# Prompt attention in one straight list with scores two steps ahead, weights and values changing places on TensorE, and DeltaNet's ScalarE work in one activation table

## What is computed

```python
def stick_breaking_block(q, k, v, q_pos, k_pos):
    z = einsum('bqhd,bshd->bhqs', q, k) * HEAD_DIM ** -0.5
    valid = k_pos[None, :] < q_pos[:, None]
    log_keep = where(valid, log_sigmoid(-z), 0)
    log_rest = cumsum(log_keep, axis=3, reverse=True) - log_keep
    a = where(valid, exp(log_sigmoid(z) + log_rest), 0)
    return einsum('bhqs,bshd->bqhd', a, v)

def trunk_layer(...):
    proj = rmsnorm(x, g_mix) @ w_in
    c = silu(causal_conv(dn_qkv));  qa, ka, va = split(c)
    qa = l2norm(qa) * HEAD_DIM ** -0.5;  ka = l2norm(ka)
    o_a, s_new = gated_delta_rule(qa, ka, va, g, beta, s0)     # in blocks along the tokens
    o_a = rmsnorm(o_a, g_out_dn) * silu(z)
    o_b = stick_breaking(rmsnorm(sb_q), concat(k_past, rmsnorm(sb_k)), concat(v_past, sb_v))
    h = x + concat(o_a, o_b) @ w_out
    h = h + square(relu(rmsnorm(h) @ w_up)) @ w_down
    return h + sigmoid(rmsnorm(h) @ w_ple_gate) * (p @ w_ple_proj)
```

## Time and profile before

| | us |
|---|---|
| median of 3 runs | 2249.35 (2248.25 to 2250.07) |
| profiled execution | 2247.63 |
| its span, first to last instruction | 2245.9 |
| prompt attention, first L1587 to first L1636 | 436.5 to 676.7 |
| DeltaNet, chunk loop and ends | about 737 to 1222 |
| one attention pair, scores at 501.75 to scores at 559.96 | 58.2 |
| one DeltaNet chunk, the load before Ln at 846.79 to the same at 901.54 | 54.75 |
| granted TensorE clock, mean | 0.944 |

### The profile page before, as it was taken

One profiled execution on the slowest core, in us unless ns is written; L12 is line 12 of the kernel. 1 busy time (PEld: TensorE's weight loads), 2 busy tenths in 40 slices (PEclk: granted clock), 3 DMA queues, 4 the chain that ended last, 5 costly groups with the idle time before them and its releaser, 6 DMA issues.

```text
span 2245.9 us, 32884 instructions
## 1 busy us (share of the span) xinstructions
PE 2010.0 (89%) x13793; PEld 1867.9 (83%) x13793; DVE 893.9 (40%) x1069; ACT 556.1 (25%) x926; POOL 607.6 (27%) x239
## 2 busy tenths in 40 slices
PE   5999999776775699999998999999999999999699
PEld 4899899644543488888887999999999999999577
DVE  5550336366662366666563152122221222225421
ACT  4231132345454233333332031001010010103210
POOL 5213323000001433333320233434334343343100
PEclk9999999888788799999997999999999999999899
DMA  5022211200004200000002011111111111111101
GB/s 166 20 76 73 82 67 57 86 1 1 1 1 155 67 20 20 19 19 19 19 9 86 20 57 38 41 36 56 56 37 43 33 56 56 37 51 47 64 28 39
DMA packets 90868, 104.16 MB, mean 46 GB/s; under 512 B 9492, under 2 KB 74336, under 8 KB 90784
## 3 DMA queue, kind: packets, MB, share of 16 engines
q1 hardware_dynamic: 81440, 89.96, 12.5%
q10 hardware_dynamic: 9344, 12.98, 1.6%
HBM read 85.32 MB, written 17.60 MB: 46 GB/s over the span
## 4 chain that ended last, share of the span: by engine, by line
PE 81%; DVE 6%; ACT 6%; issue 2%; DMA 2%; POOL 2%; SPq 0%; ACTq 0%; DVEq 0%; POOLq 0%
PE psum L1542 43%; PE psum L1514 4%; PE psum L1515 4%; PE psum L1516 4%; PE psum L1814 3%; PE psum L1818 3%; PE psum L1803 2%; PE psum L1587 2%; PE psum L1611 2%; PE psum L1737 2%; PE psum L1600 2%; DVE area L1255 1%; PE psum L1590 1%; DVE area L1160 1%; ACT area L903 1%
## 5 line engine op out<-in xcount | busy, mean ns | idle before, releaser
L674 POOL TENSOR_TENSOR w_hi<-w_raw,ones 128x2048 fp32r<-128x2048 f32 x51 | 184.7, 3622 | 1132.6 <-PE psum L1542 622.8
L1542 PE MATMUL psum<-act_hi,w_hi 128*128 128x352 f32 x1248 | 270.0, 324 | 0.6 <-ACT area L1039 0.6
L1542 PE MATMUL psum<-act_hi,w_lo 128*128 128x352 f32 x1248 | 268.9, 323 | 0.0
L1542 PE MATMUL psum<-act_lo,w_hi 128*128 128x352 f32 x1248 | 268.6, 323 | 0.0
L675 POOL TENSOR_TENSOR w_lo<-w_raw,w_hi 128x2048 fp32r<-128x2048 f32 x51 | 255.2, 5004 | 4.0
L1514 PE MATMUL psum<-w_hi,act_hi 128*128 128x256 f32 (+1 forms) x720 | 225.9, 314 | 28.2 <-issue 17.2
L1515 PE MATMUL psum<-w_lo,act_hi 128*128 128x256 f32 (+1 forms) x720 | 221.5, 308 | 0.0
L1516 PE MATMUL psum<-w_hi,act_lo 128*128 128x256 f32 (+1 forms) x720 | 220.4, 306 | 0.0
L1394 DVE TENSOR_TENSOR area<-psum,area 128x1056 f32<-128x1056 f32 x72 | 90.5, 1257 | 317.3 <-PE psum L1542 317.3
L1542 PEld LDWEIGHTS psum<-act_hi,w_lo 128*128 128x128 f32 x1248 | 214.2, 188 | 0.0
L1542 PEld LDWEIGHTS psum<-act_hi,w_hi 128*128 128x128 f32 x1248 | 212.4, 189 | 0.7 <-ACT area L1039 0.7
(11 more groups left out here) (268 smaller groups left out, 3082.1 us busy)
## 6 DMA issues: line engine op xcount, KB each, us to landing
w_raw<-in_w_up_dram SPq DMA_DIRECT2D x16, 1024.0 KB, 5.5
w_raw<-in_w_down_dram SPq DMA_DIRECT2D x16, 1024.0 KB, 5.0
w_raw<-in_w_in_dram SPq DMA_DIRECT2D x14, 1024.0 KB, 5.5
area<-in_x_prompt_dram SPq DMA_DIRECT2D x16, 512.0 KB, 4.0
conv_scratch<-area ACTq DMA_DIRECT2D x12, 512.0 KB, 2.6
area<-conv_scratch SPq DMA_DIRECT2D x8, 768.0 KB, 4.5
w_raw<-in_cache_k_dram SPq DMA_DIRECT2D x2, 2048.0 KB, 8.7
area<-in_cache_v_dram SPq DMA_DIRECT2D x2, 2048.0 KB, 8.4
```

The source lines that it names most:

```text
L674: own.link(pool.tensor_tensor(hi, w_raw[:, slot, :], ones[:, 0:1].to_broadcast([P, BLK]), ALU.mult))
L1542: last = pe.matmul(bank(base + c)[0:rows, 0:CH], w(k), a[:, k, CH * c:CH * (c + 1)], start=(k == 0 and w is lhs_hi and a is hi), stop=(k = ...
```

## The change

- The loop over pairs is gone: `STEPS` is one list of 32 (pair, tile) steps, the same tile order in each pair, written out on all engines. Semaphores count on from 0, without the 1 added at the start.
- Scores are made two steps ahead. TensorE's order is turn(s, 0), scores(s+2), values(s-1), turn_out(s-2), turn(s, 1). ScalarE's is copies(s, 0), sigmoids(s+2, 0), copies(s, 1), sigmoids(s+2, 1), copy_out(s-1). The score banks, the ring buffers and at_buf keep their size.
- In the value product the attention block is the weight matrix (128x128) and 64 columns of values stream; the output is token-major. ScalarE copies it to SBUF (`copy_out`, two buffers), TensorE transposes it (`turn_out`) into the other columns of its bank, VectorE splits that.
- DeltaNet: the table set with both Exp and Ln is loaded ahead. One over the square root in `output` is Ln and Exp on ScalarE in place of Sqrt and VectorE's reciprocal. The Exp that ends the key norm writes PSUM banks 4 and 5 in place of SBUF, and `unit_norms` reads it there.

```diff
+        ORDER = [t for n in range(NT // 2) for t in (n, NT - 1 - n)]
+        STEPS = [(i, t) for i in range(WT) for t in ORDER]
...
+        out_buf = [o_buf.rearrange("p g d -> p (g d)"), ab_raw[:, :, :].rearrange("p k c -> p (k c)")]
...
...
+            def sigmoids(step, u):
+                w = P * (STEPS[step][1] + 1)
+                act.wait_ge(scores_ready, step + 1)
+                if step >= 2:
+                    act.wait_ge(att_turned, 2 * (step - 2) + u + 1)
...
+            def copy_weights(step, u):
+                if step:
+                    act.wait_ge(o_ready, step)
                 for n, lo, hi in pieces_of(step, u):
+                    act.wait_ge(turned, n + 1)
                     act.activation(at_buf[:, u, lo:hi], bank(4 + n % 2)[:, 0:hi - lo], ACT.Copy).then_inc(att_placed, 1)
+            def copy_out(step):
+                act.wait_ge(o_ready, step + 1)
+                if step >= 2:
+                    act.wait_ge(o_turned, step - 1)
+                act.activation(out_buf[step % 2], bank(6 + step % 2)[:, 0:P], ACT.Copy).then_inc(o_copied, 1)
+            for step in range(2):
+                for u in range(2):
+                    sigmoids(step, u)
+            for step in range(len(STEPS)):
+                for u in range(2):
+                    copy_weights(step, u)
+                    if step + 2 < len(STEPS):
+                        sigmoids(step + 2, u)
+                if step:
+                    copy_out(step - 1)
+            copy_out(len(STEPS) - 1)
...
-                act.activation(rs, rs, ACT.Exp, scale=-0.5).then_inc(sd2_made, 1)
+                act.activation(head_banks(4, P, n), rs, ACT.Exp, scale=-0.5).then_inc(sd2_made, 1)
...
-                act.activation(small[0:n, 8:16], small[0:n, 0:8], ACT.Sqrt, scale=1.0 / HD,
-                               bias=eps[0:n, :]).then_inc(osd_made, 1)
+                own.link(act.activation(small[0:n, 8:16], small[0:n, 0:8], ACT.Ln, scale=1.0 / HD, bias=eps[0:n, :]))
+                act.activation(small[0:n, 48:56], small[0:n, 8:16], ACT.Exp, scale=-0.5).then_inc(osd_made, 1)
...
+            act.preload_act_table_set("natural_log_exp_and_others")
...
...
+            def split_out(step):
+                i, t = STEPS[step]
+                dve.wait_ge(o_turned, step + 1)
+                src = bank(6 + step % 2)[:, P:2 * P]
...
+            for step in range(len(STEPS)):
+                for u in range(2):
...
+                    dve.wait_ge(sig_made, 2 * step + u + 1)
...
+                if step >= 2:
+                    split_out(step - 2)
...
-                tt(d_cn[:, :, 0:n], d_c[:, 0:KT, 0:n], d_rs[:, :, 0:n], ALU.mult).then_inc(cn_made, 1)
+                tt(d_cn[:, :, 0:n], head_banks(4, P, n), d_c[:, 0:KT, 0:n], ALU.mult).then_inc(cn_made, 1)
...
-                own.link(dve.reciprocal(small[0:n, 48:56], small[0:n, 8:16]))
...
...
+            def scores(step):
...
+                if step:
+                    pe.wait_ge(sig_made, 2 * step)
...
+            def values(step):
+                i, t = STEPS[step]
+                pe.wait_ge(att_placed, pieces_of(step, 1)[-1][0] + 1)
+                if step >= 2:
+                    pe.wait_ge(o_split, step - 1)
+                for u in range(2):
+                    for n in range(t + 1):
+                        last = pe.matmul(bank(6 + step % 2)[:, HD * u:HD * (u + 1)], at_buf[:, u, P * n:P * (n + 1)],
                                          v_tok[:, n, P * i + HD * u:P * i + HD * (u + 1)],
-                                         at_buf[:, u, P * n:P * (n + 1)], start=(n == 0), stop=(n == t))
+                                         start=(n == 0), stop=(n == t))
                 last.then_inc(o_ready, 1)
...
+            def turn_out(step):
+                pe.wait_ge(o_copied, step + 1)
+                pe.transpose(bank(6 + step % 2)[:, P:2 * P], out_buf[step % 2], ident[:]).then_inc(o_turned, 1)
+            scores(0)
+            scores(1)
+            for step in range(len(STEPS)):
+                turn_weights(step, 0)
+                if step + 2 < len(STEPS):
+                    scores(step + 2)
+                if step:
+                    values(step - 1)
+                if step >= 2:
+                    turn_out(step - 2)
+                turn_weights(step, 1)
```

More of the change, by code:

```diff
@@ L447, in token_banks @@
             return psum[:, b:b + 2, :].rearrange("p a (k t) -> p (a k) t", k=4)[:, :, 0:rows]
-        UNITS = 2 * NT
-        STEPS = [t for n in range(NT // 2) for t in (n, NT - 1 - n)]
-        PIECES = 3 * NT
+        ORDER = [t for n in range(NT // 2) for t in (n, NT - 1 - n)]
+        STEPS = [(i, t) for i in range(WT) for t in ORDER]
         def columns_of(step):
-            t = STEPS[step]
+            t = STEPS[step][1]
             if t < NT // 2:
@@ L1021, in _ @@
             with act.Fori(0, (NT - 2) // 2) as i:
+                own.enter(i, 2)
                 for u in range(2):
@@ L1026, in _ @@
                     last_level(2 * i + u + 1, 1 - u)
+                own.leave((NT - 2) // 2)
             first_level(NT - 1, P)
@@ L1207, in split_out @@
                 own.link(dve.tensor_copy(dst, src))
[L1208 to L1224, removed]
+                dve.tensor_tensor(act_lo[:, WT + i, cols], src, dst.bitcast(F32), ALU.subtract).then_inc(o_split, 1)
@@ new lines, in _ @@
+            for step in range(len(STEPS)):
+                for u in range(2):
+                    w = P * (STEPS[step][1] + 1)
+                    keep, sig = keep_buf[:, u, columns_of(step)], sig_buf[:, u, columns_of(step)]
+                    dve.wait_ge(sig_made, 2 * step + u + 1)
+                    back = keep[:, ::-1]
+                    own.link(dve.tensor_tensor_scan(back, back, back, 1.0, ALU.mult, ALU.min))
+                    dve.tensor_tensor(sig[:, 0:w - 1], sig[:, 0:w - 1], keep[:, 1:w], ALU.mult).then_inc(att_made, 1)
+                if step >= 2:
+                    split_out(step - 2)
@@ L1226, in _ @@
+            split_out(len(STEPS) - 2)
+            split_out(len(STEPS) - 1)
             for g in range(2):
@@ L1603, in turn_weights @@
                 pe.sem_inc(att_turned, 1)
[L1605 to L1611, removed]
+            def values(step):
+                i, t = STEPS[step]
+                pe.wait_ge(att_placed, pieces_of(step, 1)[-1][0] + 1)
[4 more added lines that the diff above has]
+                        last = pe.matmul(bank(6 + step % 2)[:, HD * u:HD * (u + 1)], at_buf[:, u, P * n:P * (n + 1)],
                                          v_tok[:, n, P * i + HD * u:P * i + HD * (u + 1)],
-                                         at_buf[:, u, P * n:P * (n + 1)], start=(n == 0), stop=(n == t))
+                                         start=(n == 0), stop=(n == t))
                 last.then_inc(o_ready, 1)
[L1616 to L1627, removed]
+            def turn_out(step):
[12 more added lines that the diff above has]
+                turn_weights(step, 1)
+            values(len(STEPS) - 1)
+            turn_out(len(STEPS) - 2)
+            turn_out(len(STEPS) - 1)
+            pe.wait_ge(o_split, WT * NT)
             pe.wait_ge(s_staged, 4)
```

43 lines of the change are left out of this document (11 added, 32 removed).

## The result

| | before | after |
|---|---|---|
| median | 2249.61 (4 runs) | 2343.43 (2337.54 to 2347.11, 4 runs) |
| profiled execution | 2247.63 | 2345.43 |
| its span | 2245.9 | 2343.7 |
| granted TensorE clock, mean | 0.944 | 0.92 |

The ratio is 1.0416, with a 95% interval of 1.0392 to 1.0439: slower by 4.2%, some 94 us, where 40 were forecast. The time lies above the range of 2232 to 2338.

What follows compares the result with a forecast made beforehand. The prediction took waits between three engines, none full, to bound prompt attention and DeltaNet. Profiled 2247.63, + 82 for attention - 41 for DeltaNet, gave 2288.6, a median of 2290 us; range 2232 to 2338.

Steps and rivals of the forecast that it cites:

- the clock's share: Prompt attention: 0.45 of TensorE's 31.2 us of chain work a pair is paid extra for half clock, 14.0 us.
- the sum of waits: Prompt attention at full clock: 19.3 + 18.45 + 12.05 + 15.6 = 65.4 us a pair, four pairs 261.6.
- What waits for what: Prompt attention: each step lasts the larger of ScalarE's and VectorE's branches, plus scores and values in full.
- the second branch: Prompt attention: value products, turned output, split, scan, multiply, turn, scores form a chain, 18.45 us a pair in small-tile steps.
- The price of the value product: Prompt attention: 0.216 us each with attention block as weight, against 0.12 before; 72 a pair, 15.6 us against 8.9.
- VectorE's queue: Prompt attention: split_out(s-2) waits for the turned output and stands before the scans of step s+1.
- Added copy and transposition at nothing: Prompt attention: the copy of an output, 0.2 us, lies hidden under scores and values.
- DeltaNet, 41 us: DeltaNet: 5.2 us saved a chunk in seven chunks, 4.3 in the first, none in the last; bounds 28 and 51.
- My term for instruction fetch: Unrolled attention: fetching more instructions costs 0 us, bounds -1 to +3.
- The first rival: Attention serial as forecast but the clock mostly holds: attention +26 us, DeltaNet -41, total 2234; chance 0.12.
- The third: Attention: turned blocks and gaps keep the clock at half throughout, +151 - 41 us, total 2359; chance 0.07.
- The second: Attention: ScalarE never waits for products, TensorE's work sets 45 us a pair, 60 less; total 2149; chance 0.08.

Runs made afterwards that it cites:

- warm: The changed kernel plus products that nobody reads in TensorE's gaps, five after each small tile's step and three after each large one's: 2275.0 us.
- dn_warm: dn_only plus two products that nobody reads in TensorE's queue after each attention step: 2209.0 us.
- no_turn: The changed kernel without copy_out and turn_out, the split reading the token-major output from the bank: 2282.9 us.
- dn_only: The kernel before with only the DeltaNet part of the change: 2212.0 us.
- two_at: old_values plus a second buffer for the turned weights, used in turn, copies waiting for the value products of two steps ago: 2174.5 us.
- old_values: The changed kernel with values kept as the weight and no copy or turn of outputs, scores still two steps ahead: 2228.7 us.

## Why the prediction was wrong, step by step

The step that failed is the clock's share: 0.45 of TensorE's work on the chain, 56 us in the stage, where the runs show 85. Two smaller terms were off too: the sum of waits was up to 16 us short and DeltaNet's gain came out 9 smaller. With the clock's 29 that makes 54 us; the forecast lacks 53.

- **What waits for what** in the attention: right. The three longest waits are the three that were named, the second branch is on the chain, and at a clock of 1.00 a pair takes 68.3 us (warm) against a sum of 65.4. In stages that is 282 against 266, the 16 us above; some of them may be the fill's.
- **The clock's share, 0.45**: the step that failed. Forecast was a pair of 76 to 85 us and a granted clock of 0.7 to 0.8; measured were 75.6, 92.4 and 88.4 us and 0.64. A pair of after takes 90.4 (511.66 to 692.48 are two). Over the 65.4 of the sum that is 25.0 of 31.2, a share of 0.80; over warm's 68.3 it is 22.1, a share of 0.71. I had named 0.8 as the end of the range and taken the middle since I read 0.3 in the old order; dn_warm doesn't bear that reading out, so the anchor had nothing under it. Six of eight bursts in the third pair ran at 0.50 to 0.61, and a value product in them cost 0.42. That the 0.8 end gave a stage of 366 where 367.3 was measured is partly luck: its share is too high for warm's pair and its sum too low, and the two cancel.
- **The range**: its ends were added up wrong. A share of 0.3 with 41 for DeltaNet gives 2272, not 2262, and with DeltaNet's bounds 2262, not 2252. The same bounds gave 2347 at the upper end, and 2343 was measured, but the range that I stated stopped at 2338.
- **The price of the value product**, 0.216 from another stage's row: right at full clock (0.22 in warm), 0.42 in the half-clock bursts. The 72 products of the third pair took 24 us against 16 in warm. no_turn puts the exchange at 51 us, where the sum at full clock has 27; with it the stage's clock went from 0.80 to 0.72.
- **VectorE's queue**: right, and worth 63 us.
- **Added copy and transposition at nothing**: right, as far as these runs can tell (1.1 us between two stages).
- **DeltaNet, 41 us**: 35.9 in dn_only's stretch. A steady chunk was right: the norm of after takes 1.22 us, no table load is left, the chunks are 49.6 us apart (49.5 forecast), and L1261 (L1274 after) meets GpSimd's instructions as said. It took 3.58 us where it had 1.73, and the masks start at 972.73. The ends were put too high: the gain up to the second chunk's norm was 6.8 us where I had 9.5, and the last stretch lost 1.3 where I had nothing. In VectorE's timeline of after:

```profile
965.59 1.22 DVE L1268 TENSOR_TENSOR area<-psum,area 128x1024 f32<-128x1024 f32 x1 [1.90 <-ACT psum L993]
...
969.12 3.58 DVE L1274 SCALAR_TENSOR_TENSOR area<-area 64x512 f32<-64x512 f32 x2
972.73 1.29 DVE L1336 TENSOR_TENSOR area<-psum,level 128x512 f32<-128x512 f32 x2
```

  In after 32.2 came: 40.6 without the two stalls at loop turns, which made their chunks 4.2 us longer each. My term for instruction fetch, 0 with bounds -1 to +3, looked at the unrolled stretch only. If the stalls are fetches, as the nine packets for each suggest, it missed 8.4 us in a loop of another stage.
- **The drain of 1.38 us** that the Trainium skill (ScalarE: Activation LUTs, What ACT_TABLE_LOAD costs) adds to a load would, by an estimate from that figure, have added some 19 us to the gain. dn_only's 35.5 speaks against it, and so do the rows: in before Ln starts 1.30 us after its load does, and the load takes 1.28. That Exp and Ln share a set, as the same page of the Trainium skill says, is borne out: in after no load stands between them.
- **The first rival** (the clock holds) named the right term and its wrong end. **The third** (half clock all through, 2359) had the right end and went too far: two of eight bursts ran at 0.75 and 1.00. **The second** (two steps ahead as meant) fell for the reason given, the single buffer; two_at shows what it needed. The score banks, which I named beside it, didn't prevent it.

## What to carry to other kernels

Work laid further ahead helps only if every buffer between has room for it. Ask of each instruction that is moved earlier who holds the place that it will write or that its reader will write, and look for the one wait that then ends last; here one buffer was worth 51 us of a stage (old_values to two_at), and a wait in an idle engine's queue 63 us. And where TensorE works in bursts between gaps, work out its part of the chain at half clock too before choosing a share: here 0.7 to 0.8 of it was paid, while in the old order a raised clock brought 3 us.

## What the runs showed of the hardware

- Products that nobody reads, in TensorE's gaps, made the kernel 68 us faster (after to warm): the stage's granted clock rose from 0.64 to 0.97. Added to two_at the same brought 14 us (0.89 to 0.95), added to dn_only 3 (0.81 to 0.90).
- A float32 product with a 128x128 weight and 64 columns costs 0.22 us at a granted clock of 1.00 (2.4 GHz, warm) and 0.42 at 0.50 (1.2 GHz, after). One with a 128x64 weight and 128 columns, two heads side by side, costs 0.12 (before). The exchange of weight and moving operand nearly doubled the price of the same arithmetic.
- VectorE instructions with two SBUF operands took longer beside GpSimd's: L1274 3.58 us (969.12 to 972.70, beside GpSimd's L715 and L719) against 1.73 in before. With one operand in PSUM L1268 took 1.22 us beside GpSimd's L713, where L1255 of before, with two SBUF operands, took 3.2 beside a GpSimd instruction of the same length.
- In eight of thirteen kernels TensorE stood 2.3 to 3.9 us at the turn of DeltaNet's loop, with nothing in the profile that it waited for. Each such stall goes with nine more packets in the instruction queue (15, 24 and 33 packets for none, one and two).
- The same products of the last chunk ran at a granted clock of 0.51 in dn_only and of 1.00 in after.
